# Second attention's key biases as 64-row products, one head on each half of the array, and the gates' sums in every sixteenth row

## The reference

```
def shared_kv(x, kv_norm, kv_w, kv_b_f):
    proj = rmsnorm_2(x, kv_norm) @ kv_w
    k, v, f = jnp.split(proj, [D_MODEL, 2 * D_MODEL], axis=-1)
    log_f = jax.nn.log_sigmoid(f + kv_b_f)
    c = jnp.cumsum(log_f, axis=1).transpose(0, 2, 1)      # (batch, 16 heads, 512 tokens)
    return k, v, c
...
        logits = jnp.einsum('bqhd,bkhd->bhqk', qi, k)
        logits = logits + (ci[..., :, None] - c[..., None, :])
        logits = jnp.where(key_pos <= qpos, logits, -jnp.inf)
        p = jax.nn.softmax(logits, axis=-1)
        return jnp.einsum('bhqk,bkhd->bqhd', p, v)
```

## Time and profile before

| | |
|---|---|
| median of 3 runs | 2143.31 us (2141.17 to 2144.65) |
| the profiled execution | 2142.03 us, its span 2140.2 us |
| PE busy | 2066.3 us (97% of the span) |
| DVE busy | 1220.8 us (57%) |
| ACT busy | 795.5 us (37%) |
| POOL busy | 21.3 us (1%) |
| granted TensorE clock, mean | 0.987 |
| second attention | 1618 to 1699.5 us |

### The profile page before, as it was taken

The page is one execution under the profiler, slowest core; times in us unless marked ns, Lnnn a source line. Parts: engine busy times, 40 slices in busy tenths (PEclk is TensorE's granted clock), DMA queues, the critical chain, the costliest instruction groups (busy, mean ns, idle before and its releaser), DMA issues.

```text
span 2140.2 us, 25567 instructions
## 1 busy us (share of the span) xinstructions
PE 2066.3 (97%) x9936; PEld 1674.0 (78%) x9944; DVE 1220.8 (57%) x1719; ACT 795.5 (37%) x1236; POOL 21.3 (1%) x45
## 2 busy tenths in 40 slices
PE   7899999999999999999999999999999999999996
PEld 6776778888888888877788888878786678888885
DVE  5669645455444355456575564663537757647375
ACT  4239243232212133245343342442427734323242
POOL 1000000000000000000000000000000000000000
PEclk9989999999999999999999999999999999999998
DMA  4410412222222222321122223222220022222221
GB/s 168 158 60 1 128 50 93 104 99 99 99 98 99 99 98 77 120 89 59 60 98 98 98 79 113 70 94 89 99 99 21 21 79 79 98 98 98 99 83 54
DMA packets 34240, 188.52 MB, mean 88 GB/s; under 512 B 4440, under 2 KB 8696, under 8 KB 14400
## 3 DMA queue, kind: packets, MB, share of 16 engines
q1 hardware_dynamic: 31296, 179.41, 23.8%
q0 software_dynamic: 1696, 5.72, 1.0%
q10 hardware_dynamic: 1152, 2.10, 0.3%
HBM read 182.54 MB, written 2.11 MB: 86 GB/s over the span
## 4 chain that ended last, share of the span: by engine, by line
PE 88%; DVE 5%; ACT 2%; issue 1%; DVEq 1%; PEld 1%; DMA 1%; PEldq 0%; POOL 0%; SPq 0%; ACTq 0%; POOLq 0%
PE bank L409 23%; PE bank L411 23%; PE bank L410 23%; PE bank L486 4%; PE bank L491 4%; PE bank L487 4%; PE bank L1196 2%; PE bank L1166 1%; PE bank L645 1%; DVE w_lo L357 1%; PE bank L2205 1%; PE bank L1183 1%; ACT w_hi L343 1%; PE bank L2197 1%; DVEq L1238 0%
## 5 line engine op out<-in xcount | busy, mean ns | idle before, releaser
L343 ACT ACTIVATE w_hi<-w_raw 128x2048 fp32r<-128x2048 f32 (+3 forms) x174 | 314.4, 1807 | 812.0 <-PE bank L411 689.6
L409 PE MATMUL bank<-a_hi,w_hi 128*128 128x512 f32 x1376 | 540.3, 393 | 3.7 <-DVE shared L2546 1.6
L411 PE MATMUL bank<-a_hi,w_lo 128*128 128x512 f32 x1376 | 536.5, 390 | 0.0
L410 PE MATMUL bank<-a_lo,w_hi 128*128 128x512 f32 x1376 | 536.5, 390 | 0.0
L357 DVE TENSOR_TENSOR w_lo<-w_raw,w_hi 128x2048 fp32r<-128x2048 f32 (+3 forms) x174 | 374.8, 2156 | 143.7 <-ACT w_hi L343 143.5
L409 PEld LDWEIGHTS bank<-a_hi,w_hi 128*128 128x128 f32 x1376 | 258.9, 188 | 60.0 <-issue 3.4
L411 PEld LDWEIGHTS bank<-a_hi,w_lo 128*128 128x128 f32 x1376 | 258.8, 188 | 54.2
L410 PEld LDWEIGHTS bank<-a_lo,w_hi 128*128 128x128 f32 x1376 | 259.0, 188 | 53.3 <-issue 0.2
L409 PE MATMUL bank<-big_halves,w_hi 128*128 128x512 f32 x616 | 240.6, 391 | 3.1 <-DVE w_lo L357 3.0
L411 PE MATMUL bank<-big_halves,w_lo 128*128 128x512 f32 x616 | 239.8, 389 | 0.0
L410 PE MATMUL bank<-big_halves,w_hi 128*128 128x512 f32 x616 | 239.7, 389 | 0.0
(11 more groups left out here) (340 smaller groups left out, 2432.6 us busy)
## 6 DMA issues: line engine op xcount, KB each, us to landing
w_raw<-in_w_fu SPq DMA_DIRECT2D x44, 1024.0 KB, 4.8
w_raw<-in_w_up SPq DMA_DIRECT2D x16, 1024.0 KB, 4.8
w_raw<-in_w_down SPq DMA_DIRECT2D x16, 1024.0 KB, 4.8
w_raw<-in_w_fd SPq DMA_DIRECT2D x16, 1024.0 KB, 4.8
w_raw<-in_w_fd SPq DMA_DIRECT2D x8, 768.0 KB, 4.3
w_raw<-in_w_rqk SPq DMA_DIRECT2D x4, 1024.0 KB, 5.0
w_raw<-in_w_rvg SPq DMA_DIRECT2D x4, 1024.0 KB, 5.0
w_raw<-in_w_gate SPq DMA_DIRECT2D x4, 1024.0 KB, 4.8
```

What stands on the lines that cost most here:

```text
L343: act.activation(w_hi[slot][:, cols], raw[slot][:, cols], ACT.Copy).then_inc(hi_half_ready.sem if half == 0 else hi_ready.sem, 1)
L409: pe.matmul(out, w[0], x[0], start=first, stop=False)
L410: pe.matmul(out, w[0], x[1], start=False, stop=False)
L411: return pe.matmul(out, w[1], x[0], start=False, stop=last)
```

## The change

The gates' weights are repeated eight times, so that row p of the gates' sums belongs to head p mod 16; bias, sigmoid, running sum and casts are made in all 128 rows. Of these rows 0 to 15 keep part 1, rows 16 to 31 part 2, rows 32 to 47 part 3, and rows 64 to 111 the same once more; the others are multiplied by zero. Which part a row keeps comes from a constant `part_of`, and which head it belongs to from a constant `head_of`; an unused table of 128 columns goes. Each part is cast into a tile of its own and then put into `parts` by a per-row factor. The clears on POOL and the casts back to float go. The selector is written by one ACT copy. The key bias of head 0 of a pair then uses rows 0 to 63 of `sel` and `parts`, that of head 1 rows 64 to 127.

```diff
+    c["head_of"] = (p[:, None] % FH == np.arange(FH)[None, :]) & (p[:, None] % 64 < 3 * FH)
+    c["part_of"] = p[:, None] % 64 // FH == np.arange(3)[None, :]
-    c["swap_nsa"] = (p[:, None] == partner[None, :])
...
-    columns("ff", cat(kv_w[:, 2048:2064], kv_w[:, 0:112]))
+    columns("ff", cat(*[kv_w[:, 2048:2064]] * 8))
...
+            with ExitStack() as inner:
+                fx_piece = sb(inner, "fx_piece", [P, S], BF16)
...
-                        bias = sb(tmp, "fx_bias", [FH, 1])
-                        lf, t1, t2, one = (x[0:FH, :] for x in small)
+                        bias = sb(tmp, "fx_bias", [P, 1])
+                        lf, t1, t2, one = small
...
-                            dve.tensor_tensor(lf[:, :], bank[2 * slot][0:FH, :], inv[0:FH, :], ALU.mult).then_inc(evacuated.sem, 1)
+                            dve.tensor_tensor(lf[:, :], bank[2 * slot][:, :], inv[:, :], ALU.mult).then_inc(evacuated.sem, 1)
...
-                        def clear(pool):
-
-                            pool.wait_ge(hid_ready.sem, b_hid)
-                            pool.memset(parts[:, :], 0.0).then_inc(pool_step.sem, 1)
-                            pool.memset(sel[:, :], 0.0).then_inc(pool_step.sem, 1)
...
-                                rows = slice(32 * (b - 1), 32 * (b - 1) + FH)
-                                dve.tensor_copy(parts[rows, :], t1[:, :])
+                                own = const[:, at["part_of"][0] + b - 1:at["part_of"][0] + b]
+                                dve.tensor_copy(fx_piece[:, :], t1[:, :])
                                 dve.drain()
+                                if b == 1:
+                                    dve.tensor_scalar(parts[:, :], fx_piece[:, :], own, None, ALU.mult)
+                                else:
+                                    dve.scalar_tensor_tensor(parts[:, :], fx_piece[:, :], own, parts[:, :], ALU.mult, ALU.add)
                                 if b < 3:
-                                    dve.tensor_copy(t2[:, :], parts[rows, :])
-                                    dve.drain()
-                                    dve.tensor_tensor(t1[:, :], t1[:, :], t2[:, :], ALU.subtract)
-                                    dve.drain()
+                                    dve.tensor_tensor(t1[:, :], t1[:, :], fx_piece[:, :], ALU.subtract)
+                                dve.drain()
...
-                                act.wait_ge(pool_step.sem, b_pool + 2)
-                            else:
-                                rows = slice(32 * (b - 1), 32 * (b - 1) + FH)
-                                act.activation(sel[rows, :].rearrange("p (h q) -> p h q", q=P),
-                                               ident[0:FH, 0:FH, None].broadcast_to([FH, FH, P]), ACT.Copy)
+                            elif b == 1:
+                                act.activation(sel[:, :].rearrange("p (h q) -> p h q", q=P),
+                                               cst("head_of")[:, :, None].broadcast_to([P, FH, P]), ACT.Copy)
...
                     for e in range(2):
-                        head = (2 * n + e) * P
-                        pe.matmul(out[e][:, 0:w], sel[:, head:head + P], parts[:, 0:w], start=False, stop=False)
+                        rows, head = slice(64 * e, 64 * e + 64), (2 * n + e) * P
+                        pe.matmul(out[e][:, 0:w], sel[rows, head:head + P], parts[rows, 0:w], start=False, stop=False)
...
+    give("kv_b", np.tile(np.asarray(inputs["kv_b_f_2"]), 8))
```

More of the change, by code:

```diff
@@ L66, in shape_constants @@
     d = p % HD
-    partner = np.where(d < half, p + half, np.where(d < rot, p - half, p))
-    c["swap_nsa"] = (p[:, None] == partner[None, :])
+    c["head_of"] = (p[:, None] % FH == np.arange(FH)[None, :]) & (p[:, None] % 64 < 3 * FH)
+    c["part_of"] = p[:, None] % 64 // FH == np.arange(3)[None, :]
     c["swap_ret"] = (p[:, None] == ((p + RD // 2) % RD)[None, :])
@@ L2595, in bias_load @@
                         def bias_load(sp):
-                            sp.dma_start(bias[:, :], io["kv_b_f_2"].rearrange("(h a) -> h a", a=1)).then_inc(inputs_in[0].sem, 16)
+                            sp.dma_start(bias[:, :], io["kv_b"].rearrange("(h a) -> h a", a=1)).then_inc(inputs_in[0].sem, 16)
                         def v_rows(dve, grp, t):
@@ L2606, in fox @@
                         stages.append(dense("fk", two_chunks(a_tiles), scaled_to(kT), **begin))
-                        b_a, b_d, b_pool = act_step.n, dve_step.n, pool_step.n
+                        b_a, b_d = act_step.n, dve_step.n
                         sig_begin, sig_log, sig_end = log_sigmoid(lf[:, :], t1[:, :], t2[:, :], b_a, b_d)
-                        b_hid = hid_ready.n
-                        def clear(pool):
-                            pool.wait_ge(hid_ready.sem, b_hid)
-                            pool.memset(parts[:, :], 0.0).then_inc(pool_step.sem, 1)
-                            pool.memset(sel[:, :], 0.0).then_inc(pool_step.sem, 1)
                         def gate_bias(dve, b, slot, m):
@@ L2631, in gate_sums @@
                                 dve.tensor_scalar(t1[:, :], t2[:, :], -1.0, None, ALU.mult)
-                                dve.wait_ge(pool_step.sem, b_pool + 1)
                                 dve.drain()
                             else:
-                                rows = slice(32 * (b - 1), 32 * (b - 1) + FH)
-                                dve.tensor_copy(parts[rows, :], t1[:, :])
+                                own = const[:, at["part_of"][0] + b - 1:at["part_of"][0] + b]
+                                dve.tensor_copy(fx_piece[:, :], t1[:, :])
                                 dve.drain()
+                                if b == 1:
+                                    dve.tensor_scalar(parts[:, :], fx_piece[:, :], own, None, ALU.mult)
+                                else:
+                                    dve.scalar_tensor_tensor(parts[:, :], fx_piece[:, :], own, parts[:, :], ALU.mult, ALU.add)
                                 if b < 3:
-                                    dve.tensor_copy(t2[:, :], parts[rows, :])
-                                    dve.drain()
-                                    dve.tensor_tensor(t1[:, :], t1[:, :], t2[:, :], ALU.subtract)
-                                    dve.drain()
+                                    dve.tensor_tensor(t1[:, :], t1[:, :], fx_piece[:, :], ALU.subtract)
+                                dve.drain()
                         def gate_logs(act, b, slot, m):
@@ L2647, in gate_logs @@
                                 sig_log(act)
-                                act.wait_ge(pool_step.sem, b_pool + 2)
-                            else:
-                                rows = slice(32 * (b - 1), 32 * (b - 1) + FH)
-                                act.activation(sel[rows, :].rearrange("p (h q) -> p h q", q=P),
-                                               ident[0:FH, 0:FH, None].broadcast_to([FH, FH, P]), ACT.Copy)
-                        stages.append({"gpsimd": clear})
+                            elif b == 1:
+                                act.activation(sel[:, :].rearrange("p (h q) -> p h q", q=P),
+                                               cst("head_of")[:, :, None].broadcast_to([P, FH, P]), ACT.Copy)
                         act_step.n += 1
                         dve_step.n += 1
-                        pool_step.n += 2
                         stages.append(dense("ff", [[[(k * P, a_tiles[k]) for k in range(KT)]]], f_rows, gate_bias))
@@ L2763, in give @@
         io[name] = nc.dram_tensor(f"in_{name}", a.shape, mybir.dt.from_np(a.dtype), kind="ExternalInput").ap()
-    for name in ("positions", "cmp_pos_k", "cmp_pos_v", "cmp_k_w1", "cmp_k_w2", "cmp_v_w1", "cmp_v_w2", "mlstm_b_gate_2", "kv_b_f_2"):
+    for name in ("positions", "cmp_pos_k", "cmp_pos_v", "cmp_k_w1", "cmp_k_w2", "cmp_v_w1", "cmp_v_w2", "mlstm_b_gate_2"):
         give(name, np.ascontiguousarray(inputs[name]))
+    give("kv_b", np.tile(np.asarray(inputs["kv_b_f_2"]), 8))
     for name, a in packed_weights(inputs).items():
```

## The result

The changed kernel takes 2157.92 us (median of five runs; 2155.64 to 2159.01) against 2143.31 for five runs of the kernel before beside it (2141.17 to 2145.46): ratio 1.0069, 95% interval 1.0058 to 1.008. That is 0.7% slower, far above the predicted 2142.3 and outside its range of 2139.9 to 2145.6. The profiled span is 2155.5 us for 2140.2. Lines of the changed kernel are 3 higher than those of the kernel before in the parts shown here (L412 to L414 are the three products, L409 to L411 before).

What follows compares the result with a forecast made beforehand. TensorE's stream of matrix products bounds the kernel (88% of the span), with a cycle of waits in the second attention. Terms 0.84 - 1.80 = -0.96 us take 2143.31 to 2142.3, no change that can be told; range 2139.9 to 2145.6.

Steps and rivals of the forecast that it cites:

- The rest costs nothing, with its cover: Clears, selector copies, bias load and narrower table of constants: claimed to cost nothing, tenths at most for the two loads.
- Key bias pairs: Second attention: the two products of a pair overlap on opposite array halves, saving 1.80 us in all.
- The change of tile shape is moved, not added: Second attention: the 0.10 us switch from 64-row to 128-row products moves from key biases to causal bias, costing nothing.
- Rival 1: Second attention: key bias halves don't overlap; 2144.2, or 2145.6 with a second switch per unit; chance 0.09.
- The first pair: First pair of heads in the second attention: counted at nothing, at most 0.21 us saved, its waits being for staging.
- The last pair: Last pair of heads in the second attention: every unit counts; its remaining units add 0.48 us of saving.
- The waits of the cycle: Second attention: waits among PE, ACT and DVE set the turn, so only units with 512 and 128 keys count.
- Rival 2: Second attention: the whole saving counts in all eight pairs, 3.9 us; time 2139.9; chance 0.09.
- The boundary: Between value projection and output gates: part 3's added fused multiply-add makes PE wait 0.84 us more.
- Rival 3: Value projection to output gates: part 3 cast before the last evacuation, so the 0.84 us vanishes; 2141.5; chance 0.06.
- The prediction's lower figure of 0.42 us: Value projection to output gates: low bound for the fused multiply-add on bf16, 0.51 us with drain; upper bound 0.749.
- rival 4: Attention: granted clock might fall to 1.2 GHz, +5.0 us per turn; 2147.3 with one, 2152.3 with two; chance 0.03.

Runs made afterwards that it cites:

- all rows: Changed kernel with 160 unused bytes behind the table of constants and each key bias product over all 128 rows again: 2143.73 us, ratio 1.0008 to the kernel before.
- the variant with the third part moved up: Changed kernel with 160 unused bytes, third part of the gates' sums cast and added one block earlier: 2139.9 us, ratio 0.9989 to the kernel before.
- the variant with 416 bytes: Changed kernel with 416 unused bytes per partition behind the table of constants, restoring the old addresses behind it: 2143.34 us, ratio 1.0001 to the kernel before.
- 160 bytes: Changed kernel with 160 unused bytes behind the table of constants, big buffers starting at 132480: 2142.69 us against 2142.61 for the kernel before, ratio 1.0.

## Why the prediction was wrong

**The step that failed** is in "The rest costs nothing, with its cover": "The table of constants is 109 columns narrower, loaded in the first microseconds behind the first weights; nothing waits for it. Either could matter by tenths at most." I priced the table as a transfer. As an allocation it moves every tile behind it by 416 bytes, which put the big buffers 96 bytes off a multiple of 256 from the weights, and 2400 products took 0.0067 us more each. Where these products run, the changed kernel falls behind by 15.4 us in the traces. The last sentence of the prediction named moved addresses, but gave them no price and no chance. No row of the kernel before shows the price: all its products of this form lie at a distance of 0 and took the same time on either operand.

**Key bias pairs** (1.80 us less): right. The turn became 9.51 us for the forecast 9.54. The steady part of the attention gave 1.71 and 1.72. The first pair, counted at nothing with at most 0.21, gave 0.3 in the two profiles without a fall of the clock, so the attention is 2.1 us shorter. The last pair gave 0.50 us for the forecast 0.48.

**The change of tile shape is moved, not added**: right, 0.32 us from key bias to causal product for the forecast 0.33. Rival 1 is out: with all rows the 9.75 us are back.

**The waits of the cycle**: right. DVE waited 1.10 us before the first tile's maximum (1.0 or so forecast). Rival 2 is out.

**The boundary** (0.84 us more): right in kind, a little too dear. The fused multiply-add took 750 and 754 ns, the upper bound, and cast to low half became 1.32 us for 0.51. PE's wait rose by 0.70: the cast started 0.11 us sooner behind the evacuation, 0.67 us after its start for 0.78. The variant with the third part moved up confirms the place. Rival 3 is out. The prediction's lower figure of 0.42 us carried the rate of two elements a cycle over to this fused form. The Trainium skill (VectorE: DVE Perf Modes, The perf-mode tier table) gives that rate for `tensor_tensor` on bf16 and doesn't list the fused form; the 750 and 754 ns here show that it can't be carried over. The change's single-source bf16 multiply on the same shape took 354 ns.

**The clock** (rival 4): not as I had it. In the changed kernel's own profile the clock stayed at 1.00 through the attention. In other profiles the clock fell at the attention's start, in a variant of the kernel before as well, and nowhere in its steady part.

**The sum** of the change's own terms comes to +0.70 - 2.07 = -1.4 us where I had -0.96. With the addresses put right, the two ratios, 1.0001 and 1.0, can't tell it from nothing, which is what the forecast said of 0.96 us; the clock at the attention's start took it back in both profiles.

**Open** are what collides in the memory, and what settles whether the clock falls near 60 us and at the attention's start, where the change may have a share.

## What to carry to other kernels

An edit that changes the size of any allocated tile moves all tiles behind it, so print the start addresses of before and after, and take the start of the moving operand minus that of the weights for the fp32r products that fill the time: keep it at a multiple of 256 bytes, with an unused piece if need be. Only products of 128 rows and 512 columns were measured; other shapes may differ. When a kernel gets slower in stages that an edit doesn't touch, compare the same product on two operands in the groups by shape; 5 ns in 390 on one of them was 15 us here. Test a suspected address effect by moving tiles in the old kernel, code untouched.

## What the runs showed of the hardware

- 128-row fp32r products of 512 columns follow one another at 226.6 to 227.0 ns where moving operand and weights start a multiple of 256 bytes apart, at 228.6 for 64 bytes more and 233 to 235 for other multiples of 32; at 4 to 24 bytes it was 229 to 240. In whole kernels 226.7, 228.9 and 233.3. Neither start counts by itself: moving both by 32 bytes cost nothing (ratio 0.9999), moving one of them cost 15 us or, with all left operands, 47.
- bf16 products of the same shape took 215.8 ns at all 64 pairs of starts.
- Two bf16 products on opposite 64-row halves, 512 columns each, start to the next work in 0.32 us, where two on all rows took 0.44.
- The trace of a kernel whose distances are as in the kernel before can stay beside it closely: the variant with 416 bytes stayed 0.19 to 0.29 us ahead from 132 to 1530 us. Others with equal distances drifted by 0.3 us (160 bytes) and 0.5 us (all rows) between 913 and 1530 us. So a step of tenths can be read where it falls within a few microseconds, like the 0.7 at the boundary, and is the same in several profiles; over long stretches it can't.
